# Router logits from the raw residual rows: the norm's weight vector folded into the router and expert inputs, the tails of both attention layers ordered anew

## The reference, cut to what matters

```python
def rms_norm(x, g, eps=NORM_EPS):
    y = x * lax.rsqrt(jnp.mean(x * x, axis=-1, keepdims=True) + eps)
    return y * g
hp = hp + attention(rms_norm(hp, norm_mix[i]))                  # ends in "@ w_o"
h  = rms_norm(hp, norm_ffn[i])                                  # feeds router and experts
pg = softmax(h @ w_rg + b_rg); g_idx = argmax(pg)               # 4 groups
el = (h @ w_re + b_re)         # 32 experts; top 2 inside the chosen group, weights renormalised
for g in range(4):                                              # every expert e of group g
    hh = silu(h @ w_gate[g, e]) * (h @ w_up[g, e]) * gate
    y  = y + hh @ w_down[g, e]
hp = hp + y
```

## Time and profile before

| | us |
|---|---|
| median of 3 runs | 1298.98 |
| lowest, highest | 1298.47, 1306.12 |
| the profiled execution, device time | 1305.91 |
| its span, on the profiler's clock | 1304.1 |

### The profile page before, as it was taken

The page is one execution under the profiler, slowest core; times in us unless marked ns, Lnnn a source line. Parts: engine busy times, 40 slices in busy tenths (PEclk is TensorE's granted clock), DMA queues, the critical chain, the costliest instruction groups (busy, mean ns, idle before and its releaser), DMA issues.

```text
span 1304.1 us, 17890 instructions
## 1 busy us (share of the span) xinstructions
PE 1080.4 (83%) x6824; PEld 767.1 (59%) x6824; DVE 391.2 (30%) x1313; ACT 248.5 (19%) x742; POOL 281.2 (22%) x445
## 2 busy tenths in 40 slices
PE   5999999859987888469999999997867998887760
PEld 5877778735554555257686877675654554554430
DVE  2244454321211111160433333453331211211115
ACT  2134431111111011020232333321101111101101
POOL 2523230013322221220212212121002322222113
PEclk9999999969999899779999999997777999999885
DMA  9321205379999999932302121600256999999944
GB/s 306 106 66 34 99 2 197 123 256 371 373 383 382 388 385 387 321 127 75 107 18 91 58 82 58 231 29 21 91 194 233 382 372 383 390 382 377 397 149 163
DMA packets 81463, 280.03 MB, mean 215 GB/s; under 512 B 10926, under 2 KB 37630, under 8 KB 63648
## 3 DMA queue, kind: packets, MB, share of 16 engines
q1 hardware_dynamic: 63440, 231.75, 47.9%
q0 software_dynamic: 16064, 35.96, 8.5%
q10 hardware_dynamic: 1872, 11.14, 2.3%
HBM read 266.54 MB, written 28.70 MB: 226 GB/s over the span
## 4 chain that ended last, share of the span: by engine, by line
PE 59%; DMA 24%; DVE 5%; SPq 4%; issue 3%; ACT 2%; POOL 1%; POOLq 0%; ACTq 0%; DVEq 0%
PE ps L1674 20%; DMA area<-in_w_up 18%; PE ps L1952 9%; PE ps L1666 9%; PE ps L1964 4%; SPq L465 4%; DMA area<-in_w_down 2%; PE ps L1937 2%; PE ps L1682 2%; PE ps L2144 2%; PE ps L1727 2%; PE ps L1650 1%; DMA area<-hn_scratch,idx_i 1%; PE ps L2110 1%; PE ps L1849 1%
## 5 line engine op out<-in xcount | busy, mean ns | idle before, releaser
L1952 PE MATMUL ps<-area 128*64 128x256 f32 x1040 | 262.5, 410 | 62.4 <-DMA area<-in_w_up 55.1
L1674 PE MATMUL ps<-area 128*128 128x256 f32 x1152 | 279.6, 398 | 9.9 <-issue 6.1
L1953 PE MATMUL ps<-area 128*64 128x256 f32 x1040 | 263.3, 411 | 0.0
L1674 PEld LDWEIGHTS ps<-area 128*128 128x128 f32 x1152 | 223.8, 199 | 44.9 <-issue 11.7
L1952 PEld LDWEIGHTS ps<-area 128*64 128x64 f32 x1040 | 148.5, 148 | 134.9 <-issue 78.4
L613 POOL DMA_INDIRECT y_scratch<-area,idx_i x64 | 64.7, 1010 | 401.6 <-DVE area L1399 396.8
L1953 PEld LDWEIGHTS ps<-area 128*64 128x64 f32 x1040 | 148.4, 148 | 0.0
L1964 PE MATMUL ps<-area 128*64 128x512 f32 x260 | 125.4, 604 | 1.2 <-DVE area L1392 0.8
L1965 PE MATMUL ps<-area 128*64 128x512 f32 x260 | 125.4, 604 | 0.0
L1666 PE MATMUL ps<-area 128*128 128x272 f32 x512 | 123.2, 395 | 0.0
L1384 DVE TENSOR_TENSOR area<-area,ps 64x256 f32<-64x256 f32 x64 | 27.2, 425 | 297.4 <-ACT area L892 275.5
(11 more groups left out here) (216 smaller groups left out, 1104.5 us busy)
## 6 DMA issues: line engine op xcount, KB each, us to landing
area<-in_w_gate SPq DMA_DIRECT2D x65, 1024.0 KB
area<-in_w_up SPq DMA_DIRECT2D x65, 1024.0 KB
area<-in_w_down SPq DMA_DIRECT2D x65, 1024.0 KB
area<-in_w_b_qkv SPq DMA_DIRECT2D x12, 1024.0 KB
area<-y_scratch ACTq DMA_DIRECT2D x8, 1024.0 KB, 10.4
area<-in_w_a_qkv SPq DMA_DIRECT2D x6, 1024.0 KB
out<-area POOLq DMA_DIRECT2D x12, 512.0 KB, 3.5
area<-in_w_a_o SPq DMA_DIRECT2D x4, 1024.0 KB
```

The lines of the kernel that those rows point to most:

```text
L1674: ins = nc.tensor.matmul(ps[:r, bank, at_col:at_col + F], x[:, k, COL[t]:COL[t] + r], w[:, k, :], start=k == k0, stop=k == k1 - 1)
L1952: nc.tensor.matmul(ps[0:CAP, bank, 0:F], x[:, k, :], wg[:, k, :], start=k == 0, stop=k == KD - 1)
L1953: ins = nc.tensor.matmul(ps[CAP:P, bank, 0:F], x[:, k, :], wu[:, k, :], start=k == 0, stop=k == KD - 1)
```

## The change: what it does

- **Raw rows.** PE transposes `hid` itself for the router (L1665 in the new numbering, was L1650) as soon as the residual is added. The norm's vector `norm_ffn` is multiplied into the router weights once, at the start, on POOL, and the root multiplies the logits when DVE adds their bias.
- **Rows for the experts.** ACT writes `hid * rstd` to `ynorm` (`scaled_rows`) where DVE wrote `hid * rstd * g`; the vector is applied when the gathered, transposed rows are copied to `xts`, which moves from ACT to DVE as a product (L1386).
- **Router details.** The two selections are summed by PE with two matmuls in place of a DVE sum that PE waited for; the keys are multiplied into the selection matrices; the counts have their own step and go to bank 5, ahead of the last slot lists; `route_before` uses bank 4 alone.
- **Items and order.** The w_o items have new cuts, new banks (7 and 5 in place of 7 and 6) and a new order; the sample tile is one item; layer 1 starts 15 items in units 15 to 19 where it started 14; both tails are written in a new order on PE, DVE, ACT and POOL.

```diff
 def out_items(layer):
+    sample = [(4, None, 0, 8, 7)]
     if layer == 0:
-        return (first + last4 + p1(2)[:1] + p2(3, (7, 7)) + p1(2)[1:] + p2(2, (7, 6)) + full(1) + full(0))
-    return (first + p1(2) + p1(1)[:2] + last4 + p2(3, (7, 7)) + p1(1)[2:] + p2(2, (7, 7)) + p2(1, (7, 7)) + full(0))
+        t2 = full(2, (7, 7))[:2] + full(2, (5, 7))[2:]
+        return part1(3) + sample + part2(3, (7, 7)) + t2 + full(1, (5, 7)) + full(0, (5, 7))
+    return (part1(3) + part1(2)[:3] + sample + part1(2)[3:] + part1(1)[:1] + part2(3, (7, 7))[:1] + part1(1)[1:2]
+            + part2(3, (7, 7))[1:] + part1(1)[2:] + part2(2, (7, 7)) + part2(1, (5, 7)) + full(0, (5, 7)))
...
-            nc.gpsimd.tensor_copy(wr_sb[:, l, :, 0:G], stage_g[:, l])
+            nc.gpsimd.tensor_tensor(wr_sb[:, l, :, 0:G], stage_g[:, l], gT[:, l, :].unsqueeze(2).broadcast_to([P, KD, G]), ALU.mult)
...
+        def scaled_rows(n, i):
+            act.wait_ge(rstd_ready, NT * n + i + 1)
+            nc.scalar.activation(ynorm[n][i % 2][:r, :], hid[:r, t, :], ACT.Copy, scale=rstd[:r, t:t + 1]) \
+                .then_inc(y_ready, 1)
...
-                nc.scalar.activation(xts[b].rearrange("p k c -> p (k c)"), ps[:, 2 + b, :], ACT.Copy).then_inc(x_sb, 1)
+                return nc.vector.tensor_tensor(x, ps[:, bank, :].rearrange("p (k c) -> p k c", c=CAP),
+                                               gT[:, layer, :].unsqueeze(2).broadcast_to([P, KD, CAP]), ALU.mult)
...
-                own(dve, nc.vector.tensor_tensor(lg[:r, t, :], ps[:r, 2, 0:NL], br_sb[:r, layer, :], ALU.add))
+                dve.wait_ge(rstd_ready, NT * n + i + 1)
+                own(dve, nc.vector.scalar_tensor_tensor(lg[:r, t, :], ps[:r, 2, 0:NL], rstd[:r, t:t + 1],
+                                                        br_sb[:r, layer, :], ALU.mult, ALU.add))
...
-            pe.wait_ge(y_ready, NT * n + i + 1)
+            if n % 2:
+                pe.wait_ge(hid_attn, OUT_DONE[n // 2][t])
...
-            y = ynorm[n][i % 2][:r, :].rearrange("p (c k) -> p k c", k=KD)
+            y = (hid[:r, t, :] if n % 2 else ynorm[n][i % 2][:r, :]).rearrange("p (c k) -> p k c", k=KD)
...
             for e in range(NE):
                 mult(e)
+                if e + 1 < NE:
+                    x_copy(e + 1)
                 ht_copy(e)
...
-            if u >= 2:
-                pe.wait_ge(at["b", "o"], u - 1)
+            if u >= 1:
+                pe.wait_ge(at["b", "o"], u)
```

More of the change, by code:

```diff
@@ L278, in program @@
     norm_at = [R_N, R_N, R_F + 3 * SLOT, R_N, R_F + 3 * SLOT]
-    gbc = [part(a, D) for a in norm_at]
+    gT = sb("gT", [P, 2, KD])
+    gbc = {n: part(norm_at[n], D) for n in (0, 2, 4)}
     ynorm = [[part(a + D * (1 + i), D) for i in range(2)] for a in norm_at]
@@ L301, in program @@
     sofar = part(M0 + 840, NT, NE)
-    keyed = [part(M0 + 1000 + 160 * i, NT, NE) for i in range(2)]
+    shifted = part(M0 + 1000, NT, 2)
     sel = [part(M0 + 1320 + 640 * i, NT, P) for i in range(2)]
@@ L745, in _ @@
                     table(p + 1)
[L746 to L751, removed]
+            if s == UNITS - 1:
+                norm_small(3, 0)
+                norm_small(3, 1)
+                rows_out(3, 0)
+        rows_out(3, 1)
         for i in range(2, NT):
-            norm_late(1, i)
+            norm_small(3, i)
+            rows_out(3, i)
         moe(1)
@@ L861, in _ @@
                 q_copy(j + 1, i // 2)
+        square(1, 0)
         a_flip_copy(UNITS - 2)
-        square(1, 0)
-        a_flip_copy(UNITS - 1)
         square(1, 1)
         xt_copy(1, 0)
+        scaled_rows(1, 0)
+        a_flip_copy(UNITS - 1)
+        scaled_rows(1, 1)
         xt_copy(1, 1)
@@ L870, in _ @@
             xt_copy(1, i)
+            scaled_rows(1, i)
         def moe(layer):
@@ L1025, in _ @@
             pos_act_at(step, 1)
-            if step == UNITS - 1:
-                square(3, 0)
             if step >= 1:
@@ L1030, in _ @@
             pos_act_at(step, 2)
+            if step == UNITS - 2:
+                square(3, 0)
+        xt_copy(3, 0)
+        square(3, 1)
+        b_flip_copy(UNITS - 1)
         o_copy(UNITS - 2)
-        xt_copy(3, 0)
-        b_flip_copy(UNITS - 1)
-        square(3, 1)
+        scaled_rows(3, 0)
         o_squares(UNITS - 1)
+        scaled_rows(3, 1)
         xt_copy(3, 1)
+        square(3, 2)
         o_copy(UNITS - 1)
-        for i in range(2, NT):
-            square(3, i)
-            xt_copy(3, i)
+        square(3, 3)
+        xt_copy(3, 2)
+        scaled_rows(3, 2)
+        scaled_rows(3, 3)
+        xt_copy(3, 3)
+        square(3, 4)
+        xt_copy(3, 4)
+        scaled_rows(3, 4)
         moe(1)
@@ L1620, in _ @@
                 out_norm(step - 1)
-            if step == UNITS - 1:
-                y_rows(3, 0)
-            else:
-                pos_at(step, 2)
+            pos_at(step, 2)
         moe(1)
@@ L1697, in out_item @@
                 pe.wait_ge(hid_attn, OUT_BASE[layer] + earlier[-1] + 1)
[L1698 to L1699 removed]
+            elif bank == 5:
+                pe.wait_ge(ptd["ab"[layer]], (two_blocks[-1], UNITS)[layer])
             elif layer == 0:
@@ L1738, in route_before @@
                 pe.wait_ge(ptd["ab"[layer]], (two_blocks[-1], UNITS)[layer])
-            if i >= 2:
-                pe.wait_ge(r_sel, NT * layer + i - 1)
-            ins = nc.tensor.matmul(ps[:r, 4 + i % 2, 0:NE], before[:r, :r], both[:r, t, :], start=True, stop=i == 0)
+            if i >= 1:
+                pe.wait_ge(r_sel, NT * layer + i)
+            for c in range(2):
+                ins = nc.tensor.matmul(ps[:r, 4, 0:NE], before[:r, :r], hot[c][:r, t, :], start=c == 0, stop=c == 1 and i == 0)
             if i:
                 pe.wait_ge(r_sum, (NT - 1) * layer + i)
-                ins = nc.tensor.matmul(ps[:r, 4 + i % 2, 0:NE], ones[:, :r], sofar[:, i - 1, :], start=False, stop=True)
+                ins = nc.tensor.matmul(ps[:r, 4, 0:NE], ones[:, :r], sofar[:, i - 1, :], start=False, stop=True)
             ins.then_inc(r_before, 1)
```

228 lines of the change are left out of this document (107 added, 121 removed).

## The result

| | before | after |
|---|---|---|
| median of the runs beside each other | 1298.88 us (4) | 1257.19 us (4) |
| lowest, highest | 1298.47, 1306.12 | 1256.56, 1258.97 |
| profiled execution, device time | 1305.91 | 1257.34 |
| its span | 1304.1 | 1255.6 |

The ratio is 0.966, with a 95% interval of 0.9625 to 0.9694: 41.7 us less by the medians, 48.5 us by the two profiles, against 44.0 forecast. The forecast of 1255 us is 2 us under the median. By the profiles the gain was larger than the sum, and the excess has one place, as the rows show.

What follows compares the result with a forecast made beforehand. PE was taken as the main bound (59% of the chain of waits; DMA 24%, DVE 5%). Gains of 30.5 + 1.0 + 5.7 + 7.0 - 0.2 = 44.0 us from the 1298.98 us median gave 1255 us, range 1245 to 1280.

Steps and rivals of the forecast that it cites:

- T0: In each layer, SP's load issued when PE has done the last w_o item; forecast at 928.5 in layer 1.
- layer 0 up to T0: Layer 0's tail: half of PE's 1.9 us idle in 54 us goes, 1.0 us gained.
- Layer 1 up to T0: Layer 1's tail: transposes wait only for the residual, PE runs at layer 0's density and clock; T0 30.5 us earlier.
- taking the clock alike over busy and idle time: Layer 1's tail: PE's work at full clock taken as 65.48 x 0.78 = 51.1 us.
- the work summed from single rows: Layer 1's tail: bound without any idle, some 48 us of work, putting T0 at 925.
- The 1.7 us for the moved records: Eight w_o records move from layer 1's tail into units 17 and 18, where PE is full, starting the tail 1.7 us later.
- Rival B: Layer 1's tail stays loose, half of its 34 us of idle and slow clock left: 1270 us, chance 0.16.
- Rival C: Layer 1's T0 hardly moves, residual waits replacing norm waits or DVE's routing ending each wait: 1285.5 us, chance 0.05.
- The handovers: From T0 to the first gather's landing: rows, not row numbers, end the wait; 5.7 and 7.0 us gained in the layers.
- Rival A: At the first gather: it comes in with the four loads, 14.0 us instead of 7.8: 1267 us, chance 0.18.
- Rival D: In the experts: DVE's product into `xts` delays each of 64, costing 64 us against the 44: 1319 us, chance 0.03.
- One for one?: Expert stage: its end moves with the first expert, one for one, while the gap in the load stream is open.

Runs made afterwards that it cites:

- raw_old_order: The changed kernel with the items, banks and tail orders of the kernel before, keeping the raw rows: 1285.79 us, ratio 0.9855.
- keep_warm: The kernel before with identity transposes on PE ahead of each wait for the normed rows in layer 1's tail: 1301.19 us, ratio 0.9984.
- one_bank: The changed kernel with all w_o items on bank 7: 1257.35 us, ratio 0.963.
- x_behind: The changed kernel with only the two X loads held until the first gather has landed: 1256.7 us, ratio 0.9652.
- issue_first: The changed kernel with the two N and two X loads held until POOL has issued the first gather; held in layer 0 only: 1252.57 us, ratio 0.9617.
- gather_first: The changed kernel with the two N and two X loads held until the first gather has landed: 1248.22 us, ratio 0.9584.
- warm_first: As gather_first, with identity transposes on PE before and behind the last routing steps in both layers: 1248.58 us, ratio 0.9581.

## Why the prediction was right, and which terms were mis-sized

Step by step, in the two profiles (span 1304.1 and 1255.6):

| step | forecast | measured |
|---|---|---|
| layer 0 up to T0 | 1.0 | 0.4 |
| layer 0, T0 to the gather's landing | 5.7 | 5.1 |
| layer 1, start of the last unit's scores, counted from the end of layer 0's experts | -1.7 | -0.1 |
| layer 1, from there to T0 | 32.2 | 38.4 |
| layer 1, T0 to the gather's landing | 7.0 | 6.5 |
| first experts, the stages' remainders, the end | -0.2 | -1.8 |
| sum | 44.0 | 48.5 |

**Layer 1 up to T0: the mechanism was right, the size was off.** The prediction put 49.8 us of work into the stretch and a density of 54 / 52.09 on top: 51.6. Measured were 44.66 us of work in 45.44. The step that failed is "taking the clock alike over busy and idle time". PE's busy 65.3 us held about 46 us of work at the full clock (an estimate: the 44.66 measured, 1.7 for the eight records that moved, less 0.4 for the added selections), a mean of 0.70 and not 0.78. The low clock lay on busy time, as on two items of 16 records that took 6.12 and 5.39 us in place of 3.5:

```profile
935.47 6.12 PE L1674 MATMUL ps<-area 128*128 128x256 f32 x16
```

The bound named beside it, the work summed from single rows (some 48 us), was the better estimate; it only bounded the range, and the T0 of 928.5, less the 4.6 us by which layer 0's end came earlier, was 7.8 us late. The 1.7 us for the moved records was wrong as well: the layer's attention took them in at 0.1.

**Rival B** (the tail stays loose, 1270) is out: 0.78 us idle and a clock of 1.00. `raw_old_order`, 1285.8, and `keep_warm` show how near it was: raw rows without the order, or fillers without either, leave stretches of 67 and 80 us. **Rival C** (T0 hardly moves) is out with it. The Trainium skill ("TensorE: Matmul & The Clock Gate", A second HAM failure mode: psum-queue depth-cycling) blames short idles between groups that go through PSUM banks. The traces agree that short idles go with the low clock, 18.5 us of them at 0.78 against 0.8 us at 1.00. The number of banks made no difference to the changed kernel, since `one_bank` keeps 1.00; it wasn't varied in before.

**The handovers** came as written, each 0.5 to 0.6 us short. The gather's wait ends with the DMA; it is issued at T0 + 13.8 and + 13.9 (forecast 13.3); its latency is 7.87 and 7.71 (forecast 7.8). The row numbers were ready 11.6 and 11.9 us after T0 (forecast 12.0), so in neither layer were they the last thing awaited.

**Rival A** (the gather comes in with the four loads, 14.0 us) is out: 7.8 with them and 4.0 without. What was open, which loads count, is settled by `x_behind` and the two layers of `issue_first`: those issued ahead of the gather. That 7.8 was right for two loads ahead was partly luck, since it was a mean of two gathers with four loads 4 to 7 us ahead of them. The Trainium skill ("DMA: Bandwidth & Descriptors", Queues, rings and completion order) states that a transfer's semaphore increment is ordered behind the earlier writes of the same DMA engine, across queues. The runs agree on which loads count: 3.9 us for two ahead, nothing for loads behind. But a late increment isn't the whole of it, nor the most: the gather's own packets began 4.3 us after its issue, where they began 1.7 us after it without loads just in front.

**Rival D** (DVE's product into `xts` slows the experts) is out: twice the product costs 1.5 us of span, 3.1 by the medians, in place of 44.

**One for one?** The stage's end followed the first expert in the changed kernel to 0.7 and 0.5 us, and in `gather_first`, whose slot came 8.2 us earlier after T0 than before's in layer 0, to 1.3 there. `warm_first` marks the end of that: at T0 + 23.5 half of what the first expert gained was lost again.

**Against the median.** The sum was made in the profile and taken from a median of 1298.98, 7 us below that profile. By the profiles the gain is 4.5 us more than the sum, by the medians 2.3 us less. The kernel before had medians of 1302.62 to 1305.65 in the later groups, and the second bank's kernel, equal to the changed one, 1257.35 there: against those, the gain is 45 to 48 us. So the hit to 2 us is partly luck, two errors that cancel, a stretch 6 us too long and a starting point lower than most runs of before.

## What to carry to other kernels

Work at the full clock isn't busy time times the mean clock of a stretch: sum it from rows at the full clock, since the slow ones are long and the idle ones weigh nothing. Take a wait off PE by putting other work between a vector step and the matmul that needs it; filling PE in front of some of the waits brought next to nothing, since 14 of the 18.5 us of idle stayed. Where a small gather starts a stage, issue it ahead of the bulk loads: here two loads of 1 MB in front cost it 3.9 us, loads behind it nothing, but keep in front of it the loads that the stream needs: holding the four at T0 as well cost 19 us.

## What the runs showed of the hardware

- Two 1 MB loads issued 0.4 to 0.9 us ahead of a software-queue gather raised its latency from 4.0 us to between 7.7 and 8.1, and its first packets moved 4.3 us after the issue in place of 1.7; four loads of 1 MB ahead of a 512 KB write raised its time to land from 2.9 to 9.1 us, three to 8.0.
- The TensorE clock was 1.00 over 45 us with two idle pieces of 0.39 us. In before, with pieces of up to 4.0 us, its mean was 0.78, but no single piece decides: there an item of 16 records took 6.12 us after a wait of 1.25 us, and another 3.70 us after one of 1.49.
- The kernel before spread over 1296.46 to 1309.68 us in 35 runs, kernels of the changed form over 2 to 5 us each. Of the 31 beside the experiments, those under 1300 us had the higher mean granted clock, 0.920 to 0.927 against 0.913 to 0.919 over 1305 us; no profile shows where.
